# Steps 1 to 7 of a conv input projection by Strassen's scheme, seven block products for eight

## What is computed

```python
def _short_conv_layer(x, norm_g, w_in, conv_w, w_out):
    h = _rmsnorm(x, norm_g)
    proj = jnp.einsum('bsd,de->bse', h, w_in)              # w_in: 1024 x 4096
    b_g, c_g, xin, z = jnp.split(proj, 4, axis=-1)
    u = c_g * xin
    y = depthwise_causal_conv(u, conv_w)                   # 3 taps along the sequence
    y = b_g * y * jax.nn.silu(z)
    return x + jnp.einsum('bse,ed->bsd', y, w_out)

def _attn_layer(x, norm_g, w_in, b_f, q_g, k_g, w_out):
    h = _rmsnorm(x, norm_g)
    proj = jnp.einsum('bsd,de->bse', h, w_in)              # [q | k | v | gate | forget], 4096 + 16 columns
    ...                                                    # 16 heads, q and k normed, forget bias, softmax
    return x + jnp.einsum('bse,ed->bsd', o * jax.nn.silu(z), w_out)
```

## Time and profile before

| | |
|---|---|
| median of 3 runs | 1206.43 us (1206.03 to 1206.48) |
| the profiled execution | 1207.46 us |
| its span, first to last instruction | 1205.7 us |
| granted TensorE clock, mean | 0.992 |
| TensorE matmul busy | 1166.5 us (97%), 5816 matmuls |
| VectorE / ScalarE / GpSimd busy | 665.0 / 516.3 / 555.3 us |

### The profile page before, as it was taken

The page is one execution under the profiler, slowest core; times in us unless marked ns, Lnnn a source line. Parts: engine busy times, 40 slices in busy tenths (PEclk is TensorE's granted clock), DMA queues, the critical chain, the costliest instruction groups (busy, mean ns, idle before and its releaser), DMA issues.

```text
span 1205.7 us, 17301 instructions
## 1 busy us (share of the span) xinstructions
PE 1166.5 (97%) x5816; PEld 953.8 (79%) x5816; DVE 665.0 (55%) x1005; ACT 516.3 (43%) x839; POOL 555.3 (46%) x342
## 2 busy tenths in 40 slices
PE   5999999999999999899999999999999999988998
PEld 3888888888888887688787887878878878777887
DVE  7544323323324335757768677586776766866541
ACT  6311111111111212375665755757567466575510
POOL 6232322232233544457465575664665746555410
PEclk9999999999999999999999999999999999989999
DMA  6111111111111222111010100101001101002142
GB/s 209 36 53 53 52 52 35 52 52 52 35 52 70 90 86 71 35 45 36 19 36 20 35 19 16 40 31 36 18 17 35 35 18 35 18 18 70 55 159 84
DMA packets 19408, 59.76 MB, mean 50 GB/s; under 512 B 3760, under 2 KB 3760, under 8 KB 19376
## 3 DMA queue, kind: packets, MB, share of 16 engines
q1 hardware_dynamic: 19232, 59.34, 14.8%
q10 hardware_dynamic: 144, 0.00, 0.0%
HBM read 50.68 MB, written 8.65 MB: 49 GB/s over the span
## 4 chain that ended last, share of the span: by engine, by line
PE 82%; DVE 9%; issue 4%; ACT 3%; DMA 1%; POOL 0%; ACTq 0%; DVEq 0%; SPq 0%
PE ps L390 65%; PE ps L510 6%; PE ps L491 5%; PE ps L470 4%; DVE neg_max L1114 2%; DVE newton L1169 2%; DVE h_lo L978 1%; DVE newton L1165 1%; DVE newton L1167 1%; PE ps L533 1%; PE ps L474 1%; DMA x_t<-in_x 1%; DVE pt_lo L1128 1%; ACT p_small L792 0%; ACT y L906 0%
## 5 line engine op out<-in xcount | busy, mean ns | idle before, releaser
L390 PE MATMUL ps<-h_hi,w_hi 128*128 128x512 f32 x1160 | 474.9, 409 | 19.9 <-DVE h_lo L978 13.6
L390 PE MATMUL ps<-h_hi,w_lo 128*128 128x512 f32 x1160 | 455.6, 393 | 0.0
L390 PE MATMUL ps<-h_lo,w_hi 128*128 128x512 f32 x1160 | 454.0, 391 | 0.0
L1328 POOL TENSOR_TENSOR w_lo<-w_raw,w_hi 128x1024 fp32r<-128x1024 f32 x81 | 200.1, 2471 | 290.2 <-ACT w_hi L680 290.0
L390 PEld LDWEIGHTS ps<-h_hi,w_hi 128*128 128x128 f32 x1160 | 220.0, 190 | 61.1 <-DVE h_lo L978 9.3
L390 PEld LDWEIGHTS ps<-h_hi,w_lo 128*128 128x128 f32 x1160 | 218.5, 188 | 47.4
L390 PEld LDWEIGHTS ps<-h_lo,w_hi 128*128 128x128 f32 x1160 | 219.8, 189 | 35.3 <-issue 0.5
L680 ACT ACTIVATE w_hi<-w_raw 128x1024 fp32r<-128x1024 f32 x81 | 85.6, 1057 | 258.8 <-PE ps L390 256.9
L1375 POOL TENSOR_TENSOR p_big<-p_big,rdenom 128x896 f32<-128x896 f32 (+1 forms) x64 | 94.5, 1477 | 87.4 <-DVE rdenom L1122 86.8
L1114 DVE TENSOR_REDUCE neg_max<-ps 128x1 f32<-128x896 f32 (+7 forms) x128 | 96.4, 753 | 61.5 <-PE ps L474 61.0
L1128 DVE TENSOR_TENSOR pt_lo<-ps,pt_hi 128x512 fp32r<-128x512 f32 (+1 forms) x160 | 97.4, 633 | 55.4 <-ACT pt_hi L802 53.1
(11 more groups left out here) (134 smaller groups left out, 1456.7 us busy)
## 6 DMA issues: line engine op xcount, KB each, us to landing
w_raw<-in_w_cin SPq DMA_DIRECT2D x32, 512.0 KB, 3.3
w_raw<-in_w_ain SPq DMA_DIRECT2D x32, 512.0 KB, 3.3
x_t<-in_x SPq DMA_DIRECT2D x8, 512.0 KB, 9.0
w_raw<-in_w_cout SPq DMA_DIRECT2D x8, 512.0 KB, 3.3
x_dram<-x_t SPq DMA_DIRECT2D x8, 512.0 KB, 2.6
w_raw<-in_w_aout SPq DMA_DIRECT2D x8, 512.0 KB, 3.8
out<-y SPq DMA_DIRECT2D x7, 512.0 KB, 7.1
qn<-x_dram SPq DMA_DIRECT2D x4, 512.0 KB, 3.5
```

The costliest lines, as they stand in the source:

```text
L390: last = mm(ps[:, bank, :], st[:, slot, k, :], mov[:, k, halves(h)], start=(k == 0 and st is w_hi and mov is mov_hi), stop=(k == end and s ...
L1328: TT(w_lo[:, slot, :, :], w_raw[:, slot, :, :], w_hi[:, slot, :, :].bitcast(F32), ALU.subtract).then_inc(s_wlo, 1)
```

## The change

The conv projection's step 0 stays a plain product. Steps 1 to 7 use the Winograd form of Strassen's scheme: for each of two pairs of tiles `e` (C with x; gate with B) the 2x2 blocks are (tile, half of the 8 inputs) by (half of the inputs, half of the positions), and 7 products of 4 blocks replace 8. A product of 4 blocks is an "entry" of 12 matmuls. The seven data operands `b_hi[0..6]`, `b_lo[0..6]` (blocks of `h`, their sums and differences) are made once; the weight sums are made in each step by VectorE (`sums`, `late_sums`), split by ScalarE (`a_high`) and GpSimd (`a_low`) into a ring of 5 entries. Four banks for each `e` hold the products, and VectorE and ScalarE combine them when they are read.

It also changes what lies around this:
- The norm is complete before the first product: squares by ScalarE, eight float32 matmuls for the first half's sum and four (of squares added in pairs) for the second (`square_sum`), the inverse root into PSUM (`x_refine`), then `h` itself (`normed`). `inv` and L1349 are gone from the conv stage.
- `x` is reloaded from DRAM for the residual (8 more loads of 512 KB), the output projection's first four units run over `ORDER[0:6]` first.
- The forget weights' high and low parts lie side by side (`wf`, 48 columns), so that a block takes two matmuls and not three; the mean square comes behind both forget units; VectorE adds the two parts (one instruction more), ScalarE copies one.
- All loops of the conv stage are written out. Tiles have new places: `b_hi[0]` begins at byte 18976, and all of `b_hi`, `b_lo`, `a_hi`, `a_lo`, `h_hi` (18976), `h_lo0`, `h_lo1`, `w_hi0`, `w_lo0`, `w_hi1`, `w_lo1` begin 32 bytes past a multiple of 64. The attention code reads the same amounts in the same order as before.

The diff, cut to its core:

```diff
+PRODUCTS = 7
+Q, G, E, F = 0, 1, 2, 3
+BANK = (Q, G, E, Q, F, E, F)
+OPENS = (True, True, True, False, True, False, False)
+RING = 5
+ORDER = [0, 4, 1, 5, 2, 6, 3, 7]
...
+            for sp in range(1, CONV_STEPS):
+                for p in range(PRODUCTS):
+                    for e in range(2):
+                        n, done = entry(sp, p, e), group(sp, e)
+                        pe.wait_ge(s_alo, n + 1)
...
+                        if p == 3:
+                            pe.wait_ge(s_p0, done)
...
+                        if p == 5:
+                            pe.wait_ge(s_v, done)
+                        if p == 6:
+                            pe.wait_ge(s_c22, done)
+                        for k in range(KH):
+                            if e == 0 and sp == 1:
+                                pe.wait_ge(s_blo[p], (KH if p == 6 else 0) + k + 1)
+                            last = three(4 * e + BANK[p], n, p, k, OPENS[p] and k == 0, k == KH - 1)
+                        last.then_inc(s_prod, 1)
...
+            for j in range(KT):
+                square_sum(0, j, KT)
...
+            for k in range(KH):
+                pe.wait_ge(s_blo[0], k + 1)
+                for t in range(4):
...
+                    three(BANKS[t], t, 0, k, k == 0, False)
+                for j in ((0,), (1, 2, 3), (), ())[k]:
+                    square_sum(1, j, 4)
...
+            for m in range(2):
+                for h in range(2):
+                    conv_out(m, h, ORDER[0:6], True, False)
+            for m in range(2):
+                for h in range(2):
+                    conv_out(m, h, ORDER[6:8], False, True)
...
+            for sp in range(1, CONV_STEPS):
+                for q in range(PER_STEP):
+                    if q < 2:
+                        p0_copy(sp, q)
+                    if q in (6, 7):
+                        u_copy(sp, q - 6)
+                    if q == 5:
+                        gate(sp, 0)
+                    if q == 13:
+                        gate(sp, 1)
+                    a_high(entry(sp, 0, 0) + q + RING)
...
+            def x_refine(h):
+
+                dve.wait_ge(s_xln, 2 * h + 2)
+                own(TT(rs_t[:, h, :], x_g[:, h, :], x_g[:, h, :], ALU.mult))
+                own(STT(rs_t[:, h, :], ps[:, F + 4 * h, :], EPS, rs_t[:, h, :], ALU.add, ALU.mult))
+                own(STT(ps[:, F + 4 * h, :], rs_t[:, h, :], 3.0, x_g[:, h, :], ALU.subtract, ALU.mult))
...
+            for sp in range(1, CONV_STEPS):
+                c11(sp, 0)
+                c11(sp, 1)
+                for e in range(2):
+                    u_p2(sp, e)
+                c22(sp, 0)
+                c22(sp, 1)
+                if sp + 1 < CONV_STEPS:
+                    sums(sp + 1, 0)
+                else:
+                    y_low(ORDER[0])
+                    y_low(ORDER[1])
+                c12(sp, 0)
+                c12(sp, 1)
+                if sp + 1 < CONV_STEPS:
+                    sums(sp + 1, 1)
+                else:
+                    y_low(ORDER[2])
...
+                c21(sp, 0)
+                conv(sp)
+                c21(sp, 1)
+                if sp + 1 == CONV_STEPS:
+                    y_low(ORDER[6])
+                gated(sp)
+                if sp + 1 < CONV_STEPS:
+                    late_sums(sp + 1)
+            y_low(ORDER[7])
...
+            for h in range(2):
+                for k in range(KT):
+                    pe.wait_ge(s_h, 2 * k + h + 1)
+                    for mov in (hh, hl):
+                        last = mm(ps[0:3 * NH, 4 + h, :], wf[:, k, :], mov(k)[:, halves(h)],
+                                  start=(k == 0 and mov is hh), stop=(k == KT - 1 and mov is hl))
...
+            for k in range(KH):
+                t1(k)
+            for k in range(KH):
+                b_low(2, k)
+                t2(k)
+                t3(k)
+            for k in range(KH):
+                b_low(3, k)
+                t4(k)
+                b_low(4, k)
...
+            sums(1, 0)
+            sums(1, 1)
+            conv(0)
+            gated(0)
+            late_sums(1)
+            for k in range(KH):
+                b_low(6, k, 1)
...
+            def a_low(i):
+                pool.wait_ge(s_ahi, i + 1)
+                TT(a_lo[:, i % RING, :, :], entry_source(i), a_hi[:, i % RING, :, :].bitcast(F32),
+                   ALU.subtract).then_inc(s_alo, 1)
```

More of the change, by code:

```diff
@@ L23 @@
 KT = D // P
+KH = KT // 2
 NH = 16
@@ new lines, in three @@
+            def three(bank, i, b, k, first, last):
+                for st, mov in ((a_hi, b_hi[b]), (a_hi, b_lo[b]), (a_lo, b_hi[b])):
+                    ins = mm(ps[:, bank, :], st[:, i % RING, k, :], mov[:, k, :],
+                             start=(first and st is a_hi and mov is b_hi[b]),
+                             stop=(last and st is a_lo), skip_group_check=True)
+                return ins
+            pe.wait_ge(s_vconst, 1)
+            for j in range(KT):
+                square_sum(0, j, KT)
@@ L449, in scores @@
+                last.then_inc(s_unit, 1)
+            pe.wait_ge(s_xsa, 2 * KT)
+            for h in range(2):
+                mm(ps[:, 6 + h, :], mean_d[:, :], acc[:, halves(h)], start=True, stop=True).then_inc(s_ms, 1)
             def scores(it, i, par):
@@ L571, in out_ahead @@
                         pe.wait_ge(s_y2l, k // 2 + 1)
-                last = unit_part((N_AOUT + m) % 2, B_PROJ + u % 2, h, [k], h_hi, h_lo, end=KT - 2)
+                last = unit_part((N_AOUT + m) % 2, B_PROJ + u % 2, h, [k], hh, hl, end=KT - 2)
                 if k == KT - 2:
```

971 lines of the change are left out of this document (655 added, 316 removed).

## The result

The changed kernel takes 1173.59 us, median of 4 runs (1173.24 to 1174.22), against 1206.41 for the kernel before: 32.8 us less, ratio 0.9726 (95% interval 0.9713 to 0.974). The forecast was 1194.6. What came is rival A, 1174.7. The profiled execution took 1173.42, its span is 1171.6 us (before 1207.46 and 1205.7).

A forecast was written before the change was run, and what follows sets the result against it. The prediction took TensorE, 97% busy, as the bound; -18.8 through the output projection, -1.2 for forget and iteration 0 and +8.2 for attention summed to -11.8, forecasting 1194.6 us. Its own ends were 1188 and 1201; over all cases 1173 to 1203.

The forecast's parts named there:

- rival A: Both projections: data placement is free, the slow pitch on y has another cause; 1174.7 us; chance 0.24.
- What bounds the kernel now: Whole kernel: TensorE bounds it; data 32 bytes past a multiple of 64 slow the pitch from 0.2267 to 0.2343 us.
- 33/32: Projections: a row of 512 float32 beginning halfway takes 33 pieces of 64 bytes, not 32, giving 0.2338 us.
- Part 1: Conv steps 1 to 7: 168 fewer matmuls at the slower 0.2338 us pitch, -29.7 us instead of -38.1.
- Part 2: Kernel start: norm now comes first, so the first product starts near 20.4 us, at the low clock.
- Part 3: VectorE's run-up to step 1: TensorE stalls 2.5 us for u_p2, step 1 ends at 114.5; bounds none or 8 us.
- the sharp place: VectorE's run-up to step 1, where a late VectorE holds up TensorE's whole queue and counts in full.
- Part 4: Conv steps 2 to 7: no stall, 39.3 us a step, 235.7 us in all, end at 350.2.
- Rival B: Steady conv steps: VectorE and GpSimd become the bound, 43 us a step, 1220 us; chance 0.10.
- Part 5: Output projection: same 384 matmuls, 90.0 us plus 0.5 wait for the last y_lo; with the earlier parts, -18.8 us.
- Part 6: Forget part and iteration 0: 63.8 us instead of 65.0, -1.2 us.
- Part 7: Attention and output: moved h_hi and h_lo slow their matmuls, +6.6 and +1.6, together +8.2 us.

The follow-up runs named there:

- e1: Kernel before the change with 32 bytes of padding ahead of x_t, so y begins at a multiple of 64 bytes; 1205.5 us, ratio 0.9996.
- e2: Changed kernel with 32 bytes of padding ahead of a_hi and h_lo1, moving the projections' weights but not their data; 1185.6 us, ratio 0.9828.
- e3: Changed kernel with 32 bytes of padding ahead of everything, moving all data and weights together; 1174.1 us.
- e7: Changed kernel with the 24 matmuls of each step's first product issued twice, 192 a step as before the change; 1210.5 us, ratio 1.0039.
- e14: Changed kernel with 11 filler products ahead of the first sum of squares, 28 before the first product, and load_out(2) issued earlier; 1168.56 us, ratio 0.9686.
- e12: Changed kernel with six more VectorE operations of 512 columns (weight sum repeated) ahead of step 1 only; 1181.2 us.
- e8: Changed kernel with 28 filler products of mean_d before the first product and load_out(2) issued behind the second x reload; 1172.5 us.
- e18: Changed kernel with the forget part's 16 products of h_hi issued twice, 48 matmuls there as before the change; 1176.8 us.
- e13: Changed kernel with six more VectorE operations ahead of each of steps 2 to 7; 1180.3 us.
- e16: Kernel before the change with 128 bytes of padding ahead of x_t, putting weights minus y at 224 modulo 256; one execution, 1205.35 us.
- e4: Kernel before the change with 32 bytes of padding between h_lo and w_raw, moving the weights and everything behind them; 1219.8 us, ratio 1.0112.
- e5: Kernel before the change with 96 bytes of padding ahead of x_t, putting weights minus y at 0 modulo 256; 1202.5 us, ratio 0.9971.

## Why the prediction was wrong, step by step

**The step that failed** is the cause of the two pitches in "What bounds the kernel now": "I take this as the cause". The rows were right and the arithmetic, 33/32, fitted by chance; the place of the data alone decides nothing (e1, e2, e3). That "nothing else differs between rows 3 and 4" was false: the distance to the weights is 0 in one and 96 bytes in the other. It is this distance that counts, and the change has it at 0 in both projections. The forecast charged 0.0071 us on every matmul and the measured charge is none, and the one stage that had paid it before stopped paying. The text itself called the inference untested, "one case of each", and still gave it 0.58. A cause read off a single pair of stages deserved less than the null case beside it.

- **Part 1**, matmuls: forecast -29.7, with the right pitch -38.1. e7 gave them back for 36.9. This is 8.4 of the 21 us missed.
- **Part 2**, start: first product forecast at 20.4, came at 21.7. The sums took 9.06 (forecast 9.0) but began 0.9 later, as the first squares came at 5.8. Order and clock as forecast. The clock was no fixed price, though: in e14 the first product comes 1.7 earlier and the end of step 7 4.0.
- **Part 3**, run-up: forecast a stall of 2.5 at `u_p2` and step 1's end at 114.5; came waits of 0.43 in all and 113.4. Too high by 2, within its bounds of none and 8. That it is the sharp place is right (e12), but by way of the gates and `a_lo`, not of `u_p2`.
- **Part 4**, steady steps: "no stall" right, 38.1 a step instead of 39.3: 7.1 us of the miss (in part 1's sum). Rival B is refuted.
- **Part 5**, output projection: forecast 90.0 + 0.5, came 87.7 (342.00 to the first forget matmul at 429.67) with a wait of 0.6. The wait was right in size and not in cause: the last `y_low` was held up by ScalarE, which stood until 351.5 before the weights of tile 2. Their load was queued on SP behind six reloads of `x` (e8 moved it and the wait went). I had named no DMA there:

```profile
344.58 6.93 DMA raw<-in_w_cout
...
358.14 1.24 DVE b_lo L1502
359.37 0.14 issue
```

- **Part 6**: forecast 63.8, came 492.5 - 429.8 = 62.7 (rival A 62.5). e18: the 16 matmuls were worth 3.2 in the median, 3.7 in the profile.
- **Part 7**: forecast +8.2, came -2.1, which is 10.3 of the miss in the span. The -2.1 is not shown to be the change's: with the change's attention code and places, unedited, this stretch takes 678.2 us in e13 and 681.8 in e12, and with the code of before, `h` and its weights untouched, 678.8 in e16 against 681.1. The clock falls in it at places that differ from one execution to the next (before: 0.72 in 966 to 972 and 0.50 in 1074 to 1086; after: 0.50 in 1044 to 1050). The last 144 matmuls take 32.65 us, as before:

```profile
1135.82 32.65 PE ps L564 x144
```

Even with the pitch really slow this term was too big. In e4 every product of `h` there is at distance 32, the last 144 take 33.62, and from the first scores to the end it is 682.9 us: +1.7, less than the spread just told, not +8.2 and not within "4.5 to 12.1". Where 12 of these products stand together between others they take 2.85 us for 2.80, some 4 ns each and 6 us over 1500 of them, so most of that time is not on the path.

The rule of the Trainium skill (TensorE: Matmul & The Clock Gate, section Back-to-back issue gap) goes by the columns alone. On rival A's outcome it was right for this change, by the accident that all distances of the two projections are 0. The page gives its 215.8 ns for an isolated matmul and about 131 ns for a sustained stream of 512 columns; neither is in a row here, the lowest pitch of these products is 226.7, and runs e2, e4 and e5 show that placement does count.

Sum: with 0.2267 throughout and every other term kept the prediction's own rival A gives 1174.7, 1.1 from the result. The one wrong term, charged in parts 1, 4, 5, 6 and 7, made 20 of 21 us, and the range's low end, 1173, held the result only because rival A was priced.

## What to carry to other kernels

Where the same matmul has two pitches in two stages, take the addresses of both of its operands, weights too, and compare their difference modulo 256 bytes: a pad of 8 float32 moved these kernels by 12 to 13 us in the wrong direction and one of 24 by 4 in the right one. Before a forecast charges a rule inferred from one pair of rows to 1900 matmuls, price the case in which it is false as the likelier one. Where TensorE idles for some microseconds ahead of dense work, products of a constant that fill the gap can pay: behind them the first real ones started 0.227 us apart, not 0.43. And idle time of an engine is room for more work only if it lies on the right side of what others wait for: VectorE had 12 us free in a steady step, and six operations between the landing of the weights and the gates still cost TensorE 2.9 us in step 2.
